# Another load order, norm order and early table loads for four feed-forwards of a two-block layer stack

## The reference

```
def swiglu(x, w_gate, w_up, w_down):
    return (jax.nn.silu(x @ w_gate) * (x @ w_up)) @ w_down

def second_block(x, meta_tokens, ...):
    h = jnp.concatenate([meta, x], axis=1)            # 16 + 512 tokens
    for l in range(DEPTH_2):                          # 2
        h = h + 0.5 * swiglu(rmsnorm(h, ffn1_norm[l]), ffn1_w_gate[l], ffn1_w_up[l], ffn1_w_down[l])
        proj = rmsnorm(h, mix_norm[l]) @ w_in[l]
        ...                                           # y_ret, y_diff
        h = h + jnp.concatenate([y_ret, y_diff], axis=-1) @ w_out[l]
        h = h + 0.5 * swiglu(rmsnorm(h, ffn2_norm[l]), ffn2_w_gate[l], ffn2_w_up[l], ffn2_w_down[l])
    h = rmsnorm(h, final_norm)
    return h[:, N_META:]
```

## Time and profile before

| | us |
|---|---|
| median of 3 runs (lowest, highest) | 3177.53 (3172.45, 3178.45) |
| the profiled execution | 3177.6 |
| its span, first to last instruction | 3175.9 |
| TensorE busy | 3056.9 |
| VectorE, ScalarE, GpSimd busy | 2021.3, 1436.5, 172.2 |
| mean granted clock of TensorE | 0.988 |

### The profile page before, as it was taken

One profiled execution on the slowest core, in us unless ns is written; L12 is line 12 of the kernel. 1 busy time (PEld: TensorE's weight loads), 2 busy tenths in 40 slices (PEclk: granted clock), 3 DMA queues, 4 the chain that ended last, 5 costly groups with the idle time before them and its releaser, 6 DMA issues.

```text
span 3175.9 us, 55413 instructions
## 1 busy us (share of the span) xinstructions
PE 3056.9 (96%) x20248; PEld 2764.3 (87%) x20248; DVE 2021.3 (64%) x2999; ACT 1436.5 (45%) x2472; POOL 172.2 (5%) x209
## 2 busy tenths in 40 slices
PE   8999998999999899999999999999999999999997
PEld 6778785787887689999899999999999989879986
DVE  4445545773576478855566788647885566768854
ACT  3444433663343255533652455425553365246641
POOL 1000000000000011100000011001110000001100
PEclk9999999999999899999999999999999999999998
DMA  4111232222222247532121377325753212247622
GB/s 154 61 54 60 93 100 87 91 94 93 93 92 93 79 128 184 149 102 91 60 68 54 105 192 179 97 98 150 180 151 100 87 60 68 66 130 187 170 100 99
DMA packets 121787, 341.22 MB, mean 107 GB/s; under 512 B 13774, under 2 KB 13774, under 8 KB 121536
## 3 DMA queue, kind: packets, MB, share of 16 engines
q1 hardware_dynamic: 96768, 290.50, 27.2%
q0 software_dynamic: 23600, 46.87, 8.8%
q10 hardware_dynamic: 1296, 2.14, 0.2%
HBM read 337.29 MB, written 2.17 MB: 107 GB/s over the span
## 4 chain that ended last, share of the span: by engine, by line
PE 66%; issue 24%; DVE 4%; ACT 3%; DMA 2%; DVEq 1%; POOL 1%; ACTq 0%; POOLq 0%; SPq 0%
PE ps L2009 28%; PE ps L2070 9%; PE ps L2300 7%; PE ps L2303 7%; PE ps L2301 7%; PE ps L2585 3%; DMA s_raw<-in_stream 2%; PE ps L2084 1%; DVE rstd L1217 1%; PE ps L2366 1%; PE ps L2152 1%; ACT w_hi L673 1%; ACT f L875 1%; DVE w_lo L1212 1%; DVE h_lo L1223 0%
## 5 line engine op out<-in xcount | busy, mean ns | idle before, releaser
L673 ACT ACTIVATE w_hi<-w_raw 128x1024 fp32r<-128x1024 f32 x352 | 372.7, 1059 | 833.8 <-PE ps L2009 587.4
L1212 DVE TENSOR_TENSOR w_lo<-w_raw,w_hi 128x1024 fp32r<-128x1024 f32 x360 | 440.3, 1223 | 484.6 <-ACT w_hi L673 476.1
L2009 PE MATMUL ps<-f_hi,w_hi 128*128 128x264 f32 (+1 forms) x1488 | 385.7, 317 | 2.0 <-DVE f_lo L1489 2.0
L2009 PE MATMUL ps<-f_lo,w_hi 128*128 128x264 f32 (+1 forms) x1488 | 385.2, 317 | 0.0
L2009 PE MATMUL ps<-f_hi,w_lo 128*128 128x264 f32 (+1 forms) x1488 | 385.1, 316 | 0.0
L2009 PE MATMUL ps<-h_hi,w_hi 128*128 128x512 f32 (+1 forms) x896 | 303.0, 367 | 42.1 <-DVE h_lo L1223 28.5
L2009 PE MATMUL ps<-h_lo,w_hi 128*128 128x512 f32 (+1 forms) x896 | 295.8, 359 | 0.0
L2009 PE MATMUL ps<-h_hi,w_lo 128*128 128x512 f32 (+1 forms) x896 | 294.3, 358 | 0.0
L2009 PEld LDWEIGHTS ps<-f_hi,w_hi 128*128 128x128 f32 x1488 | 244.4, 188 | 22.2 <-issue 2.9
L2009 PEld LDWEIGHTS ps<-f_lo,w_hi 128*128 128x128 f32 x1488 | 245.7, 189 | 19.7
L2009 PEld LDWEIGHTS ps<-f_hi,w_lo 128*128 128x128 f32 x1488 | 245.2, 188 | 19.7
(11 more groups left out here) (365 smaller groups left out, 7489.0 us busy)
## 6 DMA issues: line engine op xcount, KB each, us to landing
w_raw<-in_stream SPq DMA_DIRECT2D x436, 512.0 KB, 3.3
s_raw<-in_stream SPq DMA_DIRECT2D x152, 256.0 KB, 4.9
s_raw<-in_stream POOLq DMA_DIRECT2D x152, 256.0 KB, 4.7
tmp<-in_stream SPq DMA_DIRECT2D x76, 256.0 KB, 5.4
xT<-in_x ACTq DMA_DIRECT2D x8, 256.0 KB, 9.7
xT<-in_x POOLq DMA_DIRECT2D x1, 2048.0 KB, 8.7
out<-tmp SPq DMA_DIRECT2D x8, 256.0 KB, 2.1
const<-in_const POOLq DMA_DIRECT2D x1, 1636.0 KB, 9.2
```

What stands on the lines that cost most here:

```text
L673: nc.scalar.activation(w_hi[:, s, :], w_raw[:, s, :], ACT.Copy).then_inc(hi_done, 1)
L1212: V.tensor_tensor(w_lo[:, s, :], w_raw[:, s, :], w_hi[:, s, :].bitcast(F32), ALU.subtract).then_inc(lo_done, 1)
L2009: last = T.matmul(out[:, p, :], w[:, s, j * P:(j + 1) * P], x[:, k, c0:c1], start=start and j == 0 and r == 0, stop=stop and j == len(ks) ...
```

## The change

It is the same arithmetic in another order, with three kinds of small additions.

- SyncE: s1, w22 and s3 of windows 0 and 1 are loaded without a wait, right behind the last plain unit and ahead of both windows' gates; in all windows s1 goes ahead of w22. The first two down units are loaded when the last two windows' gates have been split.
- ScalarE: only four of the eight scalings of `plain_h` stand ahead of `stat_root`, the others behind it. For three of the feed-forwards the upper split of the second gate unit stands ahead of `stat_root` too. In `last_pair` `down_upper(0)` is behind the copy of w22's bank.
- VectorE: of the two token sums of `t_early` the second goes to `t_late`; for three of the feed-forwards the lower split of the second gate unit is in `t_early`, ahead of the reciprocal.
- TensorE: for these three, the squares are summed behind the first unit and not inside it.
- Small additions: a Sqrt of one column ahead of the wait in `stat_root`, an Exp of one column behind `c_exps`, and on GpSimd one power of one column behind the window sums of the first feed-forward of each layer. They write to a new tile `warm` of two columns, which nobody reads.

```diff
--- before.py
+++ after.py
+        warm = alloc(ctx, "warm", [P, 2])
@@ block.sync: win_load
-                if first:
-                    sp.wait_ge(lo_done, unit - 1 - q)
-                else:
+                if not first:
                     sp.wait_ge(win_lo, 6 * (E - 2) + LO["w22"])
-                sp.dma_start(w_raw[:, q, :], gate).then_inc(wg_in[q], 16)
+                    sp.dma_start(w_raw[:, q, :], gate).then_inc(wg_in[q], 16)
+                sp.dma_start(s1_raw[:, q, :], up[:, BLK:]).then_inc(s1_base[q], 16)
                 sp.dma_start(tmp[:, 2 + q, 0:BLK], up[:, BLK:]).then_inc(w22_in[q], 16)
-                sp.dma_start(s1_raw[:, q, :], up[:, BLK:]).then_inc(s1_base[q], 16)
                 if not first:
                     sp.wait_ge(win_lo, 6 * (E - 2) + LO["s3"])
                 sp.dma_start(s3_raw[:, q, :], gate[:, 0:BLK]).then_inc(s3_base[q], 16)
@@ block.sync: ffn2_loads
                 for q in range(2):
                     win_load(which, L, q, 0, q, first=True)
+                for q in range(2):
+                    gate = 2 * (u0 + PLAIN + q)
+                    sp.wait_ge(lo_done, 2 * (u0 + PLAIN) - 1 + q)
+                    sp.dma_start(w_raw[:, q, :], stream_d[gate, :, :]).then_inc(wg_in[q], 16)
...
                 win_load(which, L, N_WIN - 1, N_WIN // 2, 0)
-                sp.wait_ge(lo_done, 2 * (u0 + FF2_TILES) - 1)
+                down = 2 * (u0 + FF2_TILES)
                 for s in range(2):
+                    sp.wait_ge(win_lo, 6 * (win_first(which, L) + N_WIN - 1 - s) + LO["w1"])
                     sp.sem_inc(w_arrived[s], 16 * N_WIN)
-                return u0 + FF2_TILES
+                    sp.dma_start(w_raw[:, s, :], stream_d[down + s, :, :]).then_inc(w_arrived[s], 16)
+                return u0 + FF2_TILES + 1
@@ block.gpsimd, in the loop over the layers
                 ffn2_sums(0, L)
+                pool.wait_ge(small_in, 16)
+                pool.drain()
+                inverse_root(warm[:, 0:1], eps, carried)
@@ block.scalar: stat_root
+                nc.scalar.activation(warm[:, 1:2], eps, ACT.Sqrt)
                 if q is None:
                     act.wait_ge(stat_ps, streamed_sums(r))
@@ block.scalar: c_exps
                 nc.scalar.activation(soft, soft, ACT.Ln, bias=1.0).then_inc(cp_done, 1)
+                nc.scalar.activation(warm[:, 1:2], eps, ACT.Exp)
@@ block.scalar: plain_h, and where the first scalings of the norms end
-            def plain_h(which, L):
+            def plain_h(which, L, ks):
...
-            plain_h(0, 0)
+            plain_h(0, 0, range(KH))
             stat_root(4, T2, 2)
@@ block.scalar: last_pair
                     for k in range(3, 5):
                         f_upper(k)
-                    after(E, "w12")
-                    down_upper(0)
                     after(E, "w22")
                     copy_out(bz, 2)
+                    down_upper(0)
@@ block.scalar: ffn2, its start and its end
-                split_hi(*following(u0, 0))
+                plain_h(which, L, range(KH, KT))
+                if (which, L) == (0, 0):
+                    split_hi(*following(u0, 0))
                 silu(0)
...
                 if which == 1 and L < LAYERS - 1:
-                    plain_h(0, L + 1)
+                    plain_h(0, L + 1, range(KH))
+                    split_hi(*following(ffn2_base(0, L + 1)[0], 0))
                 stat_root(q + 2, n_tok)
@@ block.scalar: the end of mixer
-                plain_h(1, L)
+                plain_h(1, L, range(KH))
+                split_hi(*following(ffn2_base(1, L)[0], 0))
                 stat_root(q + 2, n_out)
@@ block.vector: t_early and t_late
             def t_early(which, L):
...
                 V.tensor_tensor(f2_sums(0, hn), b11, b12, ALU.subtract).then_inc(t_sum, 1)
+                if (which, L) != (0, 0):
+                    split_lo(*following(ffn2_base(which, L)[0], 0))
+
+            def t_late(which, L):
+                hn, _, b12, b21, b22 = h_parts(ffn2_tokens(which, L))
                 dve.wait_ge(hf_done, KT * (2 * L + which) + KT)
                 V.tensor_tensor(f2_sums(1, hn), b22, b12, ALU.subtract).then_inc(t_sum, 1)
@@ block.vector: ffn2
                 plain_gate(0)
-                split_lo(*following(u0, 0))
+                if (which, L) == (0, 0):
+                    split_lo(*following(u0, 0))
                 plain_up(0)
@@ block.tensor: a step without the sum of squares
+            def h_tile(q):
+
+                def step(k):
+                    pe.wait_ge(h_lo_done, KT * q + k + 1)
+                return step
@@ block.tensor: ffn2, and the loop over the layers
                 if which == 1:
-                    first_pair(u0, g0, n_tok, at_bank, streamed(4 + 3 * L, 6 + 3 * L, n_tok))
+                    first_pair(u0, g0, n_tok, at_bank, h_tile(4 + 3 * L), lambda: sum_features(6 + 3 * L, n_tok))
...
                 if L:
-                    first_pair(*ffn2_base(0, L)[:2], T2, ffn2_banks(0, L), streamed(2 + 3 * L, 4 + 3 * L, T2))
+                    first_pair(*ffn2_base(0, L)[:2], T2, ffn2_banks(0, L), h_tile(2 + 3 * L), lambda: sum_features(4 + 3 * L, T2))
```

More of the change, by code:

```diff
@@ L870, in _ @@
             act.wait_ge(meta_in, 16)
-            def plain_h(which, L):
+            def plain_h(which, L, ks):
                 n_tok = ffn2_tokens(which, L)
                 act.wait_ge(unit_done, 2 * ffn2_base(which, L)[0])
-                for k in range(KT):
+                for k in ks:
                     nc.scalar.activation(f2[:, PLAIN + k, 0:n_tok], xT[:, k, 0:n_tok], ACT.Identity,
@@ L1515, in t_early @@
             def t_early(which, L):
-                hn, b11, b12, _, b22 = h_parts(ffn2_tokens(which, L))
+                hn, b11, b12, _, _ = h_parts(ffn2_tokens(which, L))
                 dve.wait_ge(hf_done, KT * (2 * L + which) + KH)
                 V.tensor_tensor(f2_sums(0, hn), b11, b12, ALU.subtract).then_inc(t_sum, 1)
+                if (which, L) != (0, 0):
+                    split_lo(*following(ffn2_base(which, L)[0], 0))
+            def t_late(which, L):
+                hn, _, b12, b21, b22 = h_parts(ffn2_tokens(which, L))
                 dve.wait_ge(hf_done, KT * (2 * L + which) + KT)
                 V.tensor_tensor(f2_sums(1, hn), b22, b12, ALU.subtract).then_inc(t_sum, 1)
-            def t_late(which, L):
-                hn, _, _, b21, b22 = h_parts(ffn2_tokens(which, L))
                 V.scalar_tensor_tensor(f2_sums(2, hn), f2_sums(0, hn), -1.0, b22, ALU.mult, ALU.subtract).then_inc(t_sum, 1)
```

## The result

The changed kernel takes **3143.3 us** (median of 4 runs, 3142.0 to 3144.4) against 3176.3 before; the ratio is **0.9896** (95% interval 0.9880 to 0.9912), which is 33.0 us less (28.0 to 38.1). The forecast was 3144.0, 33.6 less. The profiled execution has a span of 3142.4 us, 33.5 less than before.

A forecast was written before the change was run, and what follows sets the result against it. TensorE, busy 96% of the span, bounds the kernel; only its idle and half-clock time can be won. 4.0 + 4.3 + 8.35 + 4.5 + 4.15 + 8.3 = 33.6 off 3177.6 gives 3144.0 us, range 3138 to 3157.

The forecast's parts named there:

- Exp table: Behind the four Ln activations: the table load moves, so TensorE's four waits of 1.0 us for Exp go, 4.0 us less.
- GpSimd's power: Both mixers: an early power removes TensorE's two long waits for the eviction, 2.5 and 1.8 us, 4.3 us less.
- rival with the cold power: First power of the mixers: cold again when needed, costing 4.3 us and the clock's 2.95, 3151.3 us; chance 0.12.
- Starts: Starts of the second block's four feed-forwards, F1 to F4: TensorE resumes earlier, 2.35 us at F1, 2.0 at each other, 8.35 together.
- late split: Starts of F2 to F4: VectorE's extra large subtraction delays the next weight split, giving back 0.4 us.
- First windows and ends: Feed-forward windows: earlier loads remove waits, 4.5 us at the first windows and 4.15 at the ends of the windows.
- rival with the late gate load: Feed-forward starts: the gate's load, behind six loads, up to 3.6 us late each, 14.4 in all, 3158.4 us; chance 0.06.
- Clock: Behind removed waits at five places: falls to half clock go too, 8.3 us less.
- rival with falls elsewhere: Whole kernel: the clock falls at other places instead, so the 8.3 us isn't given back, 3152.3 us; chance 0.13.
- slower rival: Tiles behind the new one: shifted by 8 bytes, some 9,000 matmuls read more slowly, 3189 us at 5 ns each; chance 0.03.

The follow-up runs named there:

- b_tile64: The kernel before with only an unused tile of 64 bytes a partition, moving every tile behind it by 64 bytes; one run, 3177.4 us.
- b_loads: The kernel before with only the changed loads (first windows, gates, first down units) and down_upper behind the w22 copy; 3167.2 us, ratio 0.9971.
- b_exp: The kernel before with only the four small Exp activations behind the Ln ones; 3175.1 us, ratio 0.9988.
- b_power: The kernel before with only the early power on GpSimd, one per mixer, behind the window adds; 3167.5 us, ratio 0.9970.
- b_start: The kernel before with only the changed order around the norms at the feed-forward starts, without the small Sqrt; 3160.4 us, ratio 0.9950.

## Why the prediction was right, step by step

**Exp table: 4.0 forecast, 4.0 of waits measured.** The load stood in front of Exp in the trace, and the edit moved it behind Ln, where nobody waits for it. By the rule of the Trainium skill ("ScalarE: Activation LUTs", Table sets), one set for both functions, the part would be worth 0; this program disagrees, with four waits of 1.0 that went.

**GpSimd's power: 4.3 forecast, 4.3 measured.** The rival with the cold power needed something between; in the changed kernel there is nothing.

**Starts: 8.35 forecast, 9.7 measured.** TensorE's waits at the norm, the gate's eviction and the first splits were 3.7, 3.7, 4.6 and 4.1 and are 1.2, 1.3, 2.2 and 1.7. (F3 has 528 columns, as F2; only F4 has the 512 of my forecast.) The steps at F2: from the scalings to the root 4.97 us instead of 6.42, 1.45 earlier where I had 1.3; from the reciprocal to TensorE's restart 4.34 instead of 5.57, 1.23 where I had 1.1. The mis-sized term is what I gave back. I let the late split return 0.4 at each of F2 to F4 and it returns 0.2, 0.3 and 0.4; and the two steps together save 2.7 at F2 where I had 2.4.

**First windows and ends: 8.65 forecast, 8.9 measured** against the trace of before, all of both rows. But that trace was the dearest of six. In the five other executions with the old loads and the old starts these two rows are 4.1, 4.8, 6.5, 7.0 and 7.9 together; with the changed loads 0, in one execution 0.4, in one 0.7. The mean is 6.5, so the true worth is about 2 less than what one trace showed. The mechanism is as forecast: GpSimd's add for window 2 is 3.2 earlier after TensorE's restart, a little more than the 1.5 to 3 forecast. The rival with the late gate load had 3.6 at each start; none of it came, the splits of the first windows wait for no load.

**Clock: 8.3 forecast. The sum was good, the account wasn't.** I counted the five falls of one trace. Fourteen profiled executions show which of them recur (falls of the clock right behind the place, and the mean time at half clock there, over all seven):

| place | with the old code | with the edit |
|---|---|---|
| F1's start (wait 3.7, then 1.2) | 7 of 7, 4.4 us | 0 of 7 |
| F2's start (3.0, then 1.1) | 3 of 7, 1.9 us | 0 of 7 |
| F3's start (3.0, then 1.1) | 4 of 7, 2.4 us | 0 of 7 |
| F4's start (3.2, then 1.3) | 7 of 7, 3.4 us | 0 of 7 |
| end of F2's windows | 1 of 7 | 0 of 7 |
| first mixer, its powers' part | 5 of 7, 2.9 us | 2 of 7, 1.0 us |
| second mixer, the same | 4 of 7, 2.4 us | 7 of 7, 3.4 us |

b_tile64 shows it best, since its code is that of the kernel before and its tiles lie the same modulo 64. Windows view: full clock where the earlier trace rows have 0.66 at 1564 and 0.72 at 2017, and half clock at 1588, where the kernel before has no fall, and at F2's start, where the earlier trace rows have 1.00. The place at 2017 is a case of its own: the one fall stands behind a wait of 2.1 us, and in the six executions without a fall the wait there was 0.7 to 1.1.

```profile
1564.00:1574.00 10.00, 9.27 (x73) 8.13 (x73) 6.09 (x16) 7.62 (x23) 0.00 (x0) 1.00 0.16 55
1588.00:1594.00 6.00, 6.00 (x38) 6.00 (x39) 3.31 (x11) 2.85 (x9) 0.00 (x0) 0.72 0.27 90
1797.00:1806.00 9.00, 8.23 (x46) 8.27 (x47) 4.80 (x5) 1.11 (x2) 0.00 (x0) 0.64 0.35 118
2017.00:2023.00 6.00, 5.30 (x43) 5.31 (x44) 5.73 (x10) 4.64 (x9) 0.00 (x0) 1.00 0.49 175
```

At F1's and F4's starts, behind waits of 3.7 and 3.2 us, the clock fell every time; behind those of 1.0 to 3.0 in some executions and not in others. But the length of the wait alone doesn't decide. A wait of 3.2 us for o_lo near 368, which no edit touches, has a fall in 10 of the 14 executions and none in 4, and the two waits of 2.4 us for xT at the mixers' ends have one in 13 and in 7 of 14 (6 of these 7 with the old starts). Windows view right behind the wait near 368, the kernel before and b_loads:

```profile
369.00:375.00 6.00, 6.00 (x21) 4.74 (x20) 0.49 (x1) 0.00 (x0) 0.89 (x1) 0.72 0.77 259
```

```profile
369.00:375.00 6.00, 5.86 (x26) 4.86 (x27) 1.22 (x3) 0.34 (x2) 0.89 (x1) 1.00 0.70 224
```

Half of the mean time at half clock is my estimate of what a place costs. The starts give 12.1 / 2 = 6.1, where I had 3.8 from F1 and F4; I had nothing for F2 and F3, since this one trace shows no fall there. The two powers give 0.5 instead of 3.15, because in the second mixer another wait (1.0 to 1.5, for state) takes the fall over: of the rival with falls elsewhere this part is true. The end of F2's windows gives 0.2 instead of 1.4. Together 6.8 instead of 8.3. The totals agree: 74.4 us at half clock on average in the seven executions with the old starts, 59.5 in the six with all edits, and half of the difference is 7.5. The two unexplained falls of the changed kernel, near 481 and 2539, are of the same kind: none of the other thirteen executions has the first, and the second is in b_exp and b_power too.

With these means the start part alone is 9.9 (b_start's own waits) + 6.1 = 16.0; measured 15.9, with an interval that would also hold 12. The loads are 6.5 + 0.2 = 6.7; measured 9.2 (6.0 to 12.7). The power is 4.3 + 0.5 = 4.8, but measured are 9.5 (6.7 to 12.4): some 5 us of this part (2 to 8 by the interval) I can't place. Its profiled execution, 3171.3, is one of its slowest, so the trace is no help; this stays open.

**Places of the tiles: not in the sum, and close to nothing in the time.** The mechanism of my slower rival exists. It has another size, and both signs: 4.4 ns less on some 700 matmuls of f1 (3.0 us), 1.7 less on the last 570, 1.6 more on average on 400 of the merge, 1.0 more on about 1,400 in each of F1's to F3's windows. I had looked for it in a change of rate inside one trace, and one trace can't show it.

**In short.** Waits 25.3 forecast; 26.9 went at the edited places (4.0 + 4.3 + 9.7 + 8.9), and 1.3 came back in small ones elsewhere. The mechanisms were right, each shown by its own kernel, but that the total came out within 1 us is partly luck. Misjudgements offset each other: the waits in the windows (2 too many) and the counted falls (1.5 too many) were above their means, the steps at the starts (1.35) and what the power part gives (the open 5) below.

## What to carry to other kernels

Sum the waits of one trace, but before counting what chance sets (waits for loads, falls of the clock), look at several executions: here one reason's waits ran from 4 to 9 us and the time at half clock from 59 to 84 in kernels whose code was the same there. A shortened wait can be worth half a fall of the clock too, even if the trace at hand shows none: here F2's and F3's starts. And an edit that adds a tile moves all tiles behind it: keep the places fixed when parts are compared, and try a place 32 bytes on, tile by tile, since some stretches gain by it and others lose.

## What the runs showed of the hardware

- A matmul's pace depends on where the tile it reads starts. For 512 columns of f1 it is 228.9 ns at a multiple of 64 bytes and 233.3 at 32 beyond, and a shift by 64 changes nothing; for o it is 227.5 and 233.2, and a shift by 64 gives 229.2 (one execution). The windows have the opposite sign, 122.2 and 121.3, and there the matmuls that read the unmoved h change too. The Trainium skill ("Advanced Engine Details and Errata", SBUF Cachelines) has lines of 16 bytes; all these places are multiples of 16, so that rule would see no difference, and the measurement decides.
- The first power of a mixer on GpSimd waited 4.75 us in the first and 4.04 in the second mixer, where powers had run some 850 us earlier; 3.26 when an early one ran ahead of the window adds; and under 0.15 when one ran 219 us earlier with nothing between. The early power itself had its idle time, 4.5 to 9.4 us, in front of its first instruction and only some 0.15 in front of the second.
- The load of ScalarE's table ran ahead of the root's wait with or without a small activation of the same function in front of it; the difference is 0.1 us.
- The same code at the same place fell to half clock in one execution and not in the next, behind waits of 1.0 to 3.2 us. Behind the 3.2 and 3.7 of two starts it fell in seven of seven, behind another 3.2 in 10 of 14.
